# Attention on one core: v's high and low halves in one stationary tile, unscaled probabilities, and the scaling by 1/den moved to GpSimd in the pooling stage

## The reference

```python
q, k, v, u, gz = _split_ap(h @ w_in)
# attention: 8 query heads, 2 key-value heads of 64 channels, queries of a block of 128
# read 3 blocks of latent keys (|i-j| <= 128) and all 256 context keys
s = einsum('bqhgd,bkhd->bhgqk', q, k) * HEAD_DIM ** -0.5          # masked
p = softmax(concatenate([s, sink_col], -1))[..., :-1]             # a sink logit per head
attn = einsum('bhgqk,bkhd->bqhgd', p, v)
# pooling: group g takes the centred mean over w = 2, 4, 8, 16 positions minus the token
lo = clip(t - w // 2, 0, T); hi = clip(t + w // 2, 0, T)
d_g = (cs[:, hi] - cs[:, lo]) / (hi - lo) - u_g
y = concatenate([attn, (d @ pool_w) * pool_scale], -1) * silu(gz)
x = x + gate * (y @ w_out)
```

## Time and profile before

| | us |
|---|---|
| median of 3 runs | 4270.45 |
| lowest, highest | 4269.01, 4273.16 |
| span of the profiled execution | 4268.6 |
| TensorE busy | 3642.0 (85%) |
| VectorE busy | 2855.7 (67%) |
| ScalarE busy | 1513.0 (35%) |
| GpSimd busy | 359.5 (8%) |

### The profile page before, as it was taken

The page is one execution under the profiler, slowest core; times in us unless marked ns, Lnnn a source line. Parts: engine busy times, 40 slices in busy tenths (PEclk is TensorE's granted clock), DMA queues, the critical chain, the costliest instruction groups (busy, mean ns, idle before and its releaser), DMA issues. The chain is left out here.

```text
span 4268.6 us, 52411 instructions
## 1 busy us (share of the span) xinstructions
PE 3642.0 (85%) x17412; PEld 2905.4 (68%) x17412; DVE 2855.7 (67%) x4163; ACT 1513.0 (35%) x2842; POOL 359.5 (8%) x272
## 2 busy tenths in 40 slices
PE   5799969999989999489987998985899886749898
PEld 1678746777768888368866877764677775636666
DVE  6667668999910101175632179996999998868994
ACT  0343347777733323122214222213222213124553
POOL 3000060000000000000000000000000000422332
PEclk8899989999999999789998999997999998979999
DMA  7344355333222211346522213104131121143332
GB/s 275 107 119 130 99 170 97 107 111 106 86 79 81 84 66 64 122 164 217 201 96 99 82 55 109 64 35 144 65 109 65 64 78 61 60 147 117 145 137 99
DMA packets 291990, 460.86 MB, mean 108 GB/s; under 512 B 35331, under 2 KB 172291, under 8 KB 289797
## 3 DMA queue, kind: packets, MB, share of 16 engines
q1 hardware_dynamic: 267938, 420.78, 28.8%
q0 software_dynamic: 10720, 37.24, 3.2%
q10 hardware_dynamic: 13188, 0.99, 0.2%
HBM read 309.35 MB, written 149.59 MB: 108 GB/s over the span
## 5 line engine op out<-in xcount | busy, mean ns | idle before, releaser
L1046 DVE SCALAR_TENSOR_TENSOR s5b_cacc<-s5b_cu,conv_w,s5b_cacc 128x1024 f32<-128x1024 f32 x480 | 576.7, 1278 | 0.0
L160 PE MATMUL s_out_ps<-s_w_hi,s_y_hi 128*128 128x512 f32 x1024 | 420.5, 411 | 24.2 <-DVE s_y_lo L2060 21.6
L161 PE MATMUL s_out_ps<-s_w_lo,s_y_hi 128*128 128x512 f32 x1024 | 408.4, 399 | 0.0
L162 PE MATMUL s_out_ps<-s_w_hi,s_y_lo 128*128 128x512 f32 x1024 | 408.4, 399 | 0.0
L160 PE MATMUL s5b_out_ps<-s5b_xT_hi,s5b_w_hi 128*128 128x512 f32 x768 | 312.5, 407 | 62.2 <-DVE s5b_xT_lo L1267 62.2
L1046 DVE SCALAR_TENSOR_TENSOR s5a_cacc<-s5a_cu,conv_w,s5a_cacc 128x1024 f32<-128x1024 f32 x300 | 360.2, 1268 | 0.0
L1267 DVE TENSOR_TENSOR s_xT_lo<-s_xT,s_xT_hi 128x512 fp32r<-128x512 f32 x64 | 43.6, 692 | 466.6 <-ACT s_xT_hi L1226 466.6
L160 PE MATMUL s5a_out_ps<-s5a_xT_hi,s5a_w_hi 128*128 128x512 f32 x768 | 309.1, 403 | 36.6 <-DVE s5a_xT_lo L1267 36.6
L160 PE MATMUL s_out_ps<-s_xT_hi,ug_w_hi 128*128 128x512 f32 x768 | 305.6, 398 | 0.0
L162 PE MATMUL s5b_out_ps<-s5b_xT_hi,s5b_w_lo 128*128 128x512 f32 x768 | 305.2, 397 | 0.0
L161 PE MATMUL s5b_out_ps<-s5b_xT_lo,s5b_w_hi 128*128 128x512 f32 x768 | 304.8, 397 | 0.0
(11 more groups left out here) (225 smaller groups left out, 7810.2 us busy)
## 6 DMA issues: line engine op xcount, KB each, us to landing
s_k_in<-kT_d SPq DMA_DIRECT2D x32, 768.0 KB, 5.9
qT_d<-s_qk_t SPq DMA_DIRECT2D x34, 512.0 KB, 3.3
s_x<-in_x SPq DMA_DIRECT2D x16, 1024.0 KB, 6.3
s_q_in<-qT_d SPq DMA_DIRECT2D x32, 512.0 KB, 4.2
s_x<-in_x SPq DMA_DIRECT2D x32, 512.0 KB, 5.2
gT_d<-s_g_sb SPq DMA_DIRECT2D x64, 256.0 KB, 2.0
s_y<-gT_d SPq DMA_DIRECT2D x8, 2048.0 KB, 9.0
s_xr<-in_x SPq DMA_DIRECT2D x32, 512.0 KB, 4.7
```

What stands on the lines that cost most here:

```text
L160: pe.matmul(acc, lh, rh, start=first, stop=False)
L161: pe.matmul(acc, lh, rl, start=False, stop=False)
L162: return pe.matmul(acc, ll, rh, start=False, stop=last)
L1046: dve.scalar_tensor_tensor(acc, u, w, acc, ALU.mult, ALU.add).then_inc(self.step, 1)
```

## The change

Three things. First, v_hi and v_lo of a key-value head lie side by side, and are one stationary tile of 128 columns; two matmuls (with the high and the low part of the probabilities) give 128 output rows, the product with v_hi above that with v_lo (so low x low is computed too). Second, the probabilities stay unscaled: row maxima, sums and 1/den are kept for all 32 blocks, sinks are exponentiated once at the end, 1/den is transposed and stored to `rden_d`. The pooling stage loads both halves and 1/den; GpSimd adds the halves and multiplies. Third, the pooling mean multiplies by the constant 1/w inside one instruction with the subtraction; the true counts are applied to 8 tokens at either end of the sequence.

```diff
-            product(pe, o_ps[0:HD, g, :], (v[:, 0, cols], v[:, 1, cols]),
-                    (pT_hi[:, j, :], pT_lo[:, j, :]), j == 0, j == KTILES - 1).then_inc(pv_ready, 1)
+            pe.matmul(o_ps[:, g, :], v[:, g, :], pT_hi[:, j, :], start=j == 0, stop=False)
+            pe.matmul(o_ps[:, g, :], v[:, g, :], pT_lo[:, j, :], start=False, stop=j == KTILES - 1).then_inc(pv_ready, 1)
...
-                    act.activation(p_sink[:, ring, col], sink[:, h:h + 1], ACT.Exp, bias=neg_max[:, ring, col])
...
-                def scale(y, ring, i):
-                    dve.wait_ge(norm_step, 2 * y + 2)
-                    dve.tensor_scalar(probs[:, ring, i, :], probs[:, ring, i, :], rden[:, ring, i:i + 1], None, ALU.mult).then_inc(p_scaled, 1)
...
+                dve.tensor_tensor(p_sink[:], p_sink[:], p_sum[:], ALU.add).then_inc(sink_step, 1)
+                dve.wait_ge(sink_step, 3)
+                dve.reciprocal(rden[:], p_sink[:].rearrange("p b h -> p (b h)")).then_inc(rden_ready, 1)
...
-                    sp.dma_start(a_in[:], aT_d[:, cols].rearrange("(k p) t -> p k t", p=P)).then_inc(in_loaded, 16)
+                    for part in range(2):
+                        sp.dma_start(a_in[:, part], aT_d[part, :, cols].rearrange("(k p) t -> p k t", p=P)).then_inc(a_loaded, 16)
+                    for j in range(2):
+                        sp.dma_start(rd[HD * j:HD * (j + 1)], rden_d[:, cols].rearrange("(k j) t -> j k t", j=2)[j:j + 1].partition_broadcast(HD)).then_inc(a_loaded, 16)
                     sp.dma_start(u_in[:], uT_d[:, bass.ds(n * CW, UW)].rearrange("(k p) t -> p k t", p=P)).then_inc(in_loaded, 16)
-                    sp.dma_start(cnt[:], counts[:, cols].partition_broadcast(P)).then_inc(in_loaded, 16)
...
+                def attention_sum(n, k):
+                    if k == 0:
+                        pool.wait_ge(a_loaded, 64 * (n + 1))
+                    pool.tensor_tensor(a_in[:, 0, k, :], a_in[:, 0, k, :], a_in[:, 1, k, :], ALU.add).then_inc(a_step, 1)
+                    pool.wait_ge(a_step, 2 * (n * NG + k) + 1)
+                    pool.tensor_tensor(a_in[:, 0, k, :], a_in[:, 0, k, :], rd[:, k, :], ALU.mult).then_inc(a_step, 1)
...
-                    dve.tensor_tensor(src[:, at:at + CW], src[:, at:at + CW], cnt[:, g, :], ALU.mult).then_inc(sum_step, 1)
-                    dve.tensor_tensor(d[:, g % 2, :], src[:, at:at + CW], u_in[:, g, PHALO:PHALO + CW], ALU.subtract).then_inc(d_ready, 1)
+                    ins = dve.scalar_tensor_tensor(d[:, g % 2, :], src[:, at:at + CW], 1.0 / w, u_in[:, g, PHALO:PHALO + CW], ALU.mult, ALU.subtract)
```

More of the change, by code:

```diff
@@ L779, in _ @@
                     store(TILES - 1, 2 * TILES - 2 + g, g)
+                sp.wait_ge(rden_out, 1)
+                for half in range(2):
+                    sp.dma_start(rden_d[:, half * SEQ // 2:(half + 1) * SEQ // 2].rearrange("h (b t) -> b h t", t=P),
+                                 rden_T[:, half, :]).then_inc(rden_stored, 16)
+                sp.wait_ge(rden_stored, 32)
                 for g in range(2):
-                    sp.wait_ge(o_stored[g], 16 * TILES)
+                    sp.wait_ge(o_stored[g], 32 * TILES)
             @block.gpsimd
@@ L852, in _ @@
                 turn(TILES + 1, 1, 0, TILES + 1, 0, new=False, steps=2)
+                pe.wait_ge(rden_ready, 1)
+                pe.wait_ge(lo_ready, 2 * TILES * KTILES)
+                for half in range(2):
+                    ins = pe.transpose(pT_ps[:, 0, half * P:(half + 1) * P], rden[:, half * P:(half + 1) * P], ident[:])
+                ins.then_inc(rden_tr, 1)
             @block.scalar
@@ L856, in _, with exponentials @@
                 act.wait_ge(fixed_loaded, 64)
-                def exponentials(y, ring, g, i, yb):
+                def exponentials(b, y, ring, g, i, yb):
                     e = y * GRP + i
@@ L951, in turn @@
                             split_lo(y - 2, g, i - 1)
[L952 to L953 removed]
                         if new and i < GRP:
                             maxima(y, ring, i)
[L957 to L966 removed]
+                            negate(b, y, ring, g, i)
                 def body(b, slot, before, after):
@@ L1387, in build @@
             HEAD, TAIL = 2, 2
-            SUM_STEPS = sum(len(bin(w)) - 3 for w in POOL_WINDOWS) + NG
+            SUM_STEPS = sum(len(bin(w)) - 3 for w in POOL_WINDOWS)
             @block.sync
@@ L1460, in _, with body @@
                 chunks(pe, body, NCH, HEAD, TAIL)
+            @block.gpsimd
+            def _(pool):
+                def attention_sum(n, k):
[4 more added lines that the diff above has]
+                    pool.tensor_tensor(a_in[:, 0, k, :], a_in[:, 0, k, :], rd[:, k, :], ALU.mult).then_inc(a_step, 1)
+                def body(n, slot, before, after):
+                    for k in range(NG):
+                        attention_sum(n, k)
+                chunks(pool, body, NCH, HEAD, TAIL)
             @block.scalar
@@ L1503, in gate_attention, with pool_mean @@
                         dve.wait_ge(g_loaded[slot], 8 * (n + 2 - slot))
-                    dve.tensor_tensor(y[:, slot, k, :], y[:, slot, k, :], a_in[:, k, :], ALU.mult).then_inc(y_ready, 1)
-                def pool_mean(n, g, before):
-                    step = n * SUM_STEPS + sum(len(bin(w)) - 3 for w in POOL_WINDOWS[:g]) + g
+                    dve.wait_ge(a_step, 2 * (n * NG + k + 1))
+                    dve.tensor_tensor(y[:, slot, k, :], y[:, slot, k, :], a_in[:, 0, k, :], ALU.mult).then_inc(y_ready, 1)
+                def pool_mean(n, g, before, after):
+                    step = n * SUM_STEPS + sum(len(bin(w)) - 3 for w in POOL_WINDOWS[:g])
                     w = POOL_WINDOWS[g]
@@ L2132 @@
     arrays["rope"] = rope_tables()
-    arrays["counts"] = pool_counts()
+    arrays["counts"] = pool_edges()
     arrays["masks"] = band_masks()
```

153 lines of the change are left out of this document (80 added, 73 removed).

## The result

The changed kernel takes 4263.06 us (median of 12 runs, 4251.96 to 4274.54), the kernel before 4271.91 (12 runs, 4268.26 to 4275.70): a ratio of 0.9974, 95% interval 0.9967 to 0.9982. Faster, but by 9 us and not by 50, and outside the range that was given. The profiled execution (span 4251.1 us) is one of the shortest of the twelve: measured against the profile of before it gains 17.5 us, of which the other runs keep about half.

What follows compares the result with a forecast made beforehand. TensorE was taken as the bound in the attention stage, but barely, with a VectorE-ScalarE loop close behind. 63 + 12 - 2 - 23 = 50 us less, 4270 - 50 = 4220 us; range 4200 to 4240, wider 4185 to 4250.

Steps and rivals of the forecast that it cites:

- GpSimd beside VectorE in the six steady chunks: Pooling stage, six chunks other than 0 and 1: GpSimd's operations hold VectorE, costing 1.2 us of TensorE's time per chunk, 7 us.
- That bound (-45): Pooling stage's lower bound, against -23 us forecast: stalls over 3 us in each chunk, bringing the half-speed restart, some 1.6 us more.
- two signs of being wrong: Pooling stage: TensorE's waits for the d lo part pass 3 us; or attention stage: less than 50 us shorter.
- Rival (c): Pooling stage: late GpSimd becomes the bound, TensorE halts every chunk; decides from 9 us per chunk, 4285 us at 11; 4%.
- Steady turns: Attention stage, 51 turns (half a block, one key-value head each): from 9.23 to 8.0 us, 63 us less.
- today's 0.44 us of starvation: Attention stage: TensorE's idle time per turn before the change, carried over unchanged: 7.59 + 0.4 = 8.0 us.
- Rival (b): Attention stage: the VectorE-ScalarE loop replaces TensorE as bound; negation and exponential hold the turn at 8.7 us; 4260 us; 15%.
- First turns: Attention stage, first 11 turns: 12 us less, bounds 0 to 20, from a held scaling removed and key loads arriving late.
- End of the stage: End of the attention stage: added reciprocal, transposes, evacuation and stores cost 2 us, bounds 1 to 4.
- The 128-column tile: Attention stage, values product: loading a stationary tile 128 instead of 64 columns wide costs nothing, covered by the moving stream.
- Chunk 0 and 1: Pooling stage's edge chunks: 8 us lost in each, of which 5.7 us from six GpSimd operations meeting VectorE.
- Transfers and counts: Pooling stage, chunks 0 and 1: unhidden transfers cost 3.5 us each; multiplications saved give back 1.1 and 1.4 us.

## Why the prediction was wrong

**The failed step is GpSimd beside VectorE in the six steady chunks**: "as the first product needs only group 0, I take 1.2 us of TensorE's time per chunk, 7 us." It measured 29.0 us, 4.8 per chunk. Everything up to that sentence was near: GpSimd started 4.6 us ahead of VectorE's chunk (5 forecast), each held operation cost 0.9 to 1.1 us (0.95 forecast), five of them lay in the two critical groups (four forecast). Then I took less than my own sum gave. TensorE issues the products of groups 0 and 1 0.70 us after each other (1953.01 and 1953.71 in the kernel before), so group 1 counts in full, and its slack was 1.4 us (its lo part ended at 1952.35). 4.85 us held in the groups, about 1.2 in the splits of y before them, less 1.46 for two multiplications saved and 1.36 of slack: 3.2 us, and the six waits are 3.3 on average (20.1 us together). The rest of the 29.0, 1.5 us per chunk, is the slow return of TensorE (1.5 to 2.6 us by its spacings), which I had priced rightly, but only for "stalls over 3 us in each chunk", at the bottom of the bound. That bound (-45) was near the truth (-48). Of the two signs of being wrong that I had named one appeared: four of the six waits passed 3 us (2.53 to 4.18). The other did not: the attention stage got 66 us shorter, not less than 50.

**Rival (c)**, at 4%, named what TensorE does, a halt at the pooling products in every chunk and a return at half speed. Its reason was another: GpSimd late, and VectorE's gating waiting for its results. With that dependence cut the operations stay as long as they were. Its point of decision (9 us per chunk) was not reached; 41.4 us over eight chunks were enough to eat the gain. Its argument against, that GpSimd starts before VectorE's chunk does, was true and of no use: it ended 8 us into it.

**Steady turns**: the mechanism was right, the size too large (45.4 instead of 63). The wrong term was "so I carry today's 0.44 us of starvation over": it measured 8.34 - 7.56 = 0.78. The round of two steps is as fast as I computed (3.34 us: maxima 939.45, 941.12, 942.79), the negation 0.95 us behind its maximum as forecast. What costs is the fifth step's order on ScalarE; with a faster TensorE it leaves less time to catch up. Rival (b) had the right engines, VectorE and ScalarE, and the wrong reason: it held the turn at 8.7 by negation and exponential, and 8.34 lies as near to my 8.0. That its time of 4260 us is 3 us from the measured median is luck: against the two profiles it gains 18 us too little in the steady turns and 12 in the first ones, and loses 25 too little in the pooling stage.

**First turns**: 20 us instead of 12, at the upper bound; the long turn among them was 17.5 us here and 16.3 before, so the gain came from the others. **End of the stage**: the wide reciprocal took 1.75 us, near my upper bound, and still 0.6 us were gained. **The 128-column tile** costs nothing, as read: two values matmuls follow each other after 0.32 us, and the turn with the swap is TensorE's plain sum.

**Chunk 0 and 1**: GpSimd 6.0 and 6.2 us (5.7 each forecast), right. Transfers and counts were each mis-sized, 23.8 and 17.0 us, and nearly cancel: net +6.8 where I had 7.0 - 2.5 = +4.5.

**The range** ended at 4250. The steady turns as they turned out and the pooling stage at the lower bound that I had written down myself give 4270 - 45 - 12 + 2 + 45 = 4260: two terms off in the same direction, one within its bounds and one at the end of them, were enough to leave it. The median run is another 10 us longer than the profiled one (4263.06 against 4252.68 us), for which no cause is shown.

## What to carry to other kernels

Price work given to GpSimd by what it does to VectorE's duration, operation by operation, and look for a stage in which VectorE is idle, not for one in which GpSimd is. When a bound engine is relieved, read which instruction of the next one stands in front of what is awaited; a swap of two ScalarE instructions was worth 0.78 us of a turn here, and the matmuls removed only 0.40 without it. And where a working of several terms ends in a rounded-down number, keep the sum.

## What the runs showed of the hardware

- Sharing was a loss for both: GpSimd's eight operations took 13.3 us (1899.57 to 1912.82) where at 1.26 us each, as the first of them took in chunk 0, they would take 10.1, and each that met VectorE cost it about 1 us; the same eight on VectorE alone take 8 x 0.69 = 5.5 us.
- Small VectorE operations are held as long as large ones: a 128x8 product beside GpSimd took 1.11 us, and 0.17 without (VectorE's timeline of the changed kernel, chunk 0):

```profile
1757.61 1.11 DVE L1553 TENSOR_TENSOR s_edge<-s_sums,s_cnt 128x8 f32<-128x8 f32 x1
...
1766.64 0.17 DVE L1553 TENSOR_TENSOR s_edge<-s_sums,s_cnt 128x8 f32<-128x8 f32 x1
```

- A first matmul of 0.50 us after a wait is not yet a fast return. Of the six waits of chunks 2 to 7 three ended so and three with 0.80, not in the order of their lengths (2.85 us gave 0.50 at 1863.54, 2.53 gave 0.80 at 2072.41), but after all six some 7 to 12 starts lay 0.43 us apart; behind a first 0.50 they only begin two to four matmuls later. TensorE's timeline of the changed kernel:

```profile
1968.83 0.50 PE L161 MATMUL s_pool_ps<-s_d_hi,s_pw_hi 128*128 128x512 f32 x1 [4.18 <-DVE s_d_lo L1563]
...
1969.64 0.39 PE L161 MATMUL s_out_ps<-s_w_hi,s_y_hi 128*128 128x512 f32 x1
...
1970.67 0.63 PE L161 MATMUL s_out_ps<-s_w_hi,s_y_hi 128*128 128x512 f32 x1
```

- The length of the wait alone doesn't tell whether the slow stretch comes: in the kernel with GpSimd on its own tile a wait of 2.58 us (to 1916.20) was followed by none, and others of 2.58 us were; after the waits of 1.03 to 1.55 us with the work on VectorE none came. I have no reading that does.
